# A streaming encoder layer on one core: tile 0's expert routing moved into the attention stage, conditioning vectors loaded as rows, one load of the final norm, h2 of tiles 5 to 7 from the router's buffer, tile 5 routed five slots later

## Chip, cores and metric

One core of a Trainium2 chip. The metric is the device time of one launch in microseconds, the median over repeated runs. Everything is float32. The engines are PE (matrix products), DVE (vector), ACT (scalar functions), POOL (general; here it issues the gathers) and SP (here it issues DMAs); each works through its own instruction list in order and waits on semaphores.

## What is computed

One layer over 1024 prompt tokens and 32 sample tokens, D = 1024, in nine tiles of 128 tokens (the ninth holds the 32 sample tokens):

```python
sh1, sc1, g1, sh2, sc2, g2 = split(silu(c) @ w_ada + b_ada)      # per request group
h  = rmsnorm(x, norm1) * (1 + sc1) + sh1
columns = h @ w_in                                               # 1024 x 3592, to both mixers
A  = gated DeltaNet(columns)          # 4 heads, chunked delta rule, depthwise convolution in front
B  = differential attention(columns)  # 4 heads, causal by chunks of 64
x1 = x + g1 * (concat(A, B) @ w_out)
h2 = rmsnorm(x1, norm2) * (1 + sc2) + sh2
# experts: 16384 single neurons, 8 product-key heads, 16 best each
q = h2 @ peer_wq;  scores = q . peer_keys (two halves of 128 keys per head)
idx, gate = best 16 of the 16 x 16 sums of the halves' best 16;  gate = softmax
y = sum over the 128 chosen of gate * gelu(u[idx] . h2) * v[idx]
out = rmsnorm(x1 + g2 * y, final_norm)
```

The outputs are the normalised rows, the new keys and values, and the DeltaNet and convolution states.

## The kernel before

**Stages.** `build` (line 2988) emits blocks that run one after the other: `condition` (line 120: modulation vectors, 1/rms of x, load of w_in into SBUF), `project` (257: h @ w_in and the convolution for tiles 0 to 4), `deltanet` (464, tiles 0 to 4), `attend_first` (2903: attention, w_out and x1 of tiles 0 to 4) and `stream` (2858). All engines meet at the end of a block, and SP then clears the block's semaphores.

**Condition.** SP loads c_prompt, c_sample, b_ada and norm1 column-wise (lines 148 to 151: element k*128 + p goes to partition p), then w_ada in 12 column blocks of 2.1 MB through three buffers (157). PE multiplies the two conditions with each block (229) and transposes the result into columns (220). ACT squares the tiles of x (176), and from the third block on loads w_in in eight row blocks of 128 x 3592 (198); the projection's first product waits for all eight (409), then runs over eight column groups of 512 (405; the eighth has 8 columns).

**Attention.** `Attention` (1012) and `Router` (1500) are written as generators, one per engine and part, that yield a due time in planner units before each piece; `weave` (981) merges them into one instruction order per engine. In `attend_first` head n of the 20 is due at 13 + 7.5 n, the store of x1 of tile tl (1138) at 37.5 units after its last head. SP's order holds the query and key rows of the next tile (1119), the DeltaNet rows (1125), x (1131) and that store. PE: transposes of queries and keys (1295, 1296), scores (1312), transposes of the probabilities (1333), values (1348), the output projection (1376). PSUM banks 2 to 7 are used.

**Stream.** `Experts` (1803) computes 8 x 128 + 32 slots, one expert per token in each: POOL gathers a row of u and of v per token (1867, 1870; 0.5 MB each, 5 and 8 buffers), DVE multiplies u with h2 and sums (2032), ACT applies gelu (1951) and builds a diagonal matrix of the coefficients (1941), PE adds diag x v to two PSUM banks (1986). Here due times are slots; PE runs four slots behind. Beside tiles 0 to 3's slots, other stages are woven in through `Stream` (2819), one after the other: routing of tiles 0 to 4; projection (slot 145), DeltaNet (292) and attention (427) of tiles 5 to 8; from slot 604 on routing of tiles 5 to 8. Stage n's instructions wait until SP has ended stage n - 1.

**Router**, per tile: SP loads x1 into `h2r` (1546), with the first tile of a stage also the keys (1548), modulation rows (1537) and peer_wq, 8.4 MB (1551). ACT, DVE and ACT normalise `h2r` in place (1586 to 1592), DVE scales and shifts (1687, 1690), SP stores it to `h2_scratch` (1556). PE transposes the keys once (1625) and h2 (1632), multiplies with peer_wq in four blocks (1655, banks 4 and 5) and the keys (1641, banks 2 and 3), ACT copies both results out (1600, 1605), DVE finds the best keys (1697 to 1717), the candidates (1725 to 1758) and the indices (1779 to 1789). `route_*` place step p of 128 of a route between its first and last slot, w0 + p (w1 - w0)/128. Tile 0 has the slots before 0, so all of it stands ahead of the first gather; tile t of 1 to 4 has 31.5 (t - 1) and 54 slots, tiles 5 to 8 the slots of the tile before, tile 5 from 604 to 640.

**Around a tile.** POOL loads h2 of the next tile from `h2_scratch` 16 slots ahead (1848); for tiles 0 and 5 to 8 ACT copies it to PSUM at the tile's first slot (1947). At the end of a tile POOL loads x1 into `x1e` (1886), ACT squares the sum into the same buffer (1961), then POOL loads final_norm there (1889) and DVE multiplies (2072).

## Time and profile before

| | us |
|---|---|
| median of 3 runs | 4339.26 (4335.96 to 4350.27) |
| the profiled execution's own time | 4341.6 |
| its span, first to last instruction | 4339.9 |
| conditioning, up to the projection's first matmul | 152.8 |
| attention of tiles 0 to 4, SP's first load of x to the last store of x1 | 650.1 to 861.1 |
| routing of tile 0, up to the first gather | 868.1 to 965.2 |
| slots and what is woven into them | 965.2 to 4339.9 |

The span runs from the first to the last instruction; the time adds start and end of the launch. Busy shares over the span: PE 78%, DVE 57%, POOL 53%, PE's weight loads 41%, ACT 25%. The DMA engines moved 1308 MB, 1127 MB of them on POOL's queue. The share of busy time is a mean over stages with different limits, so a part is to be read in its own stretch. The granted clock is that of PE; 1.00 is 2.4 GHz and 0.50 is 1.2 GHz.

### The profile page before, as it was taken

Reading aid. Unit: us, or ns where it says so; the run is one execution under the profiler, and the core shown is the slowest. Engines: PE = TensorE matmul, PEld = TensorE weight load, DVE = VectorE, ACT = ScalarE, POOL = GpSimd, SP = SyncE. Lnnn points to the kernel's source line nnn. Section 1 sums busy time; section 2 is a strip of 40 time slices with the busy share of each in tenths; the row PEclk is TensorE's granted clock in tenths of the full one; section 3 lists DMA queues with packets and bytes.
Section 4 is the critical chain, followed back from the end, with each engine's and each line's share of the span. In section 5 each row is a group of like instructions: output and inputs, shape, how many; then the busy total and the mean of one; then the engine's idle time right before and its main releaser. Section 6 shows DMA issues by size and latency. Waiting matters only on the chain.

```text
span 4339.9 us, 37765 instructions
## 1 busy us (share of the span) xinstructions
PE 3391.8 (78%) x11402; PEld 1785.9 (41%) x11402; DVE 2489.9 (57%) x5734; ACT 1106.3 (25%) x2931; POOL 2309.2 (53%) x2237
## 2 busy tenths in 40 slices
PE   6797877638888779987986789787697788778755
PEld 1343764335555334433553344335253344235222
DVE  0132644356888766546775577654756646745653
ACT  1122334212221244112332345322211121121111
POOL 0000310006666756676777676675766666666674
PEclk9899988869999889998998899998899899899898
DMA  9322211049888989999999999999999999999996
GB/s 363 132 106 100 103 60 56 29 149 356 317 322 321 364 314 368 401 374 359 339 365 355 375 350 339 347 341 367 335 376 371 365 388 370 361 384 360 359 355 263
DMA packets 387978, 1308.12 MB, mean 301 GB/s; under 512 B 51348, under 2 KB 55684, under 8 KB 385735
## 3 DMA queue, kind: packets, MB, share of 16 engines
q0 software_dynamic: 309808, 1127.00, 69.5%
q1 hardware_dynamic: 74904, 157.12, 9.9%
q10 hardware_dynamic: 3072, 21.66, 1.3%
q8 instruction: 92, 1.51, 0.1%
q14 instruction: 102, 0.84, 0.1%
HBM read 1270.94 MB, written 38.99 MB: 302 GB/s over the span
## 4 chain that ended last, share of the span: by engine, by line
PE 33%; POOL 13%; issue 12%; DMA 11%; DVE 8%; ACT 2%; another core or an unknown queue 1%; SPq 0%; DVEq 0%; ACTq 0%; POOLq 0%
PE PS L1986 21%; DMA ubuf<-in_peer_u,idx 8%; POOL vbuf L1870 7%; POOL ubuf L1867 6%; PE PS L1655 5%; DVE ubuf L2032 3%; PE PS L2310 2%; PE PS L1376 1%; PE PS L1312 1%; PE PS L2307 1%; DMA ckeys<-rest_scratch 1%; PE PS L1641 1%; ACT diag L1941 1%; PE PS L1348 0%
## 5 line engine op out<-in xcount | busy, mean ns | idle before, releaser
L1986 PE MATMUL PS<-vbuf,diag 128*128 128x512 f32 x3936 | 1979.7, 644 | 537.6 <-issue 247.2
L1870 POOL DMA_INDIRECT vbuf<-in_peer_v,idx x1024 | 1079.8, 1054 | 733.1 <-PE PS L1986 368.3
L1986 PEld LDWEIGHTS PS<-vbuf,diag 128*128 128x128 f32 x3936 | 766.1, 206 | 1488.2 <-issue 1174.9
L1867 POOL DMA_INDIRECT ubuf<-in_peer_u,idx x1024 | 1074.3, 1049 | 389.0 <-issue 301.7
L2032 DVE SCALAR_TENSOR_TENSOR ubuf<-ubuf,PS 128x1024 f32<-128x1024 f32 x544 | 662.9, 1220 | 560.3 <-DMA ubuf<-in_peer_u,idx 414.9
L2032 DVE SCALAR_TENSOR_TENSOR ubuf<-ubuf,h2e 128x1024 f32<-128x1024 f32 x512 | 624.6, 1224 | 393.4 <-DMA ubuf<-in_peer_u,idx 339.5
L1951 ACT ACTIVATE acts<-dots 128x2 f32<-128x2 f32 x528 | 107.1, 203 | 2013.5 <-DVE ubuf L2032 1207.7
L1941 ACT ACTIVATE diag<-ident,coef 128x128 f32<-128x128 f32 x984 | 339.1, 387 | 26.7 <-PE PS L1986 21.8
L1655 PEld LDWEIGHTS PS<-h2T,wq 128*128 128x128 f32 x2304 | 290.2, 194 | 96.5 <-issue 84.8
L1655 PE MATMUL PS<-h2T,wq 128*128 128x128 f32 x2304 | 292.9, 277 | 9.6 <-ACT h2T L1595 8.5
L405 PE MATMUL PS<-w_in_sb,hT 128*128 128x512 f32 (+1 forms) x640 | 252.8, 554 | 4.0 <-DVE hT L426 2.8
L405 PEld LDWEIGHTS PS<-w_in_sb,hT 128*128 128x128 f32 x640 | 116.2, 191 | 138.0 <-issue 137.0
L610 POOL MEMSET tri<- 128x128 f32 x1 | 0.2, 205 | 286.4 <-POOLq L99 286.4
L1376 PE MATMUL PS<-wout,mT 128*128 128x512 f32 x288 | 138.6, 618 | 8.7 <-ACT mT L1246 7.3
L1840 POOL DMA_DIRECT2D g<-modrows_scratch x2 | 1.3, 668 | 225.8 <-POOLq L99 225.8
L229 PE MATMUL PS<-wada,cS 128*2 128x512 f32 x192 | 92.0, 636 | 36.6 <-DMA wada<-in_w_ada 36.6
L2310 PE MATMUL PS<-wst,hT 128*128 128x512 f32 x256 | 119.3, 597 | 0.0
L1312 PE MATMUL PS<-KT,qz 128*128 128x512 f32 (+3 forms) x224 | 98.5, 555 | 10.5 <-DVE sc L1424 7.8
L1951 ACT ACT_TABLE_LOAD x81 | 103.9, 1283 | 1.3
L642 POOL TENSOR_TENSOR lb<-bm,lvl 128x512 f32<-128x512 f32 x35 | 51.0, 1490 | 90.5 <-PE PS L743 77.4
L2003 DVE TENSOR_TENSOR coef<-acts,gate 128x2 f32<-128x2 f32 x512 | 81.5, 159 | 26.8 <-ACT acts L1951 21.7
L2015 DVE SCALAR_TENSOR_TENSOR yacc<-vbuf,coef,yacc 128x1024 f32<-128x1024 f32 x68 | 87.4, 1285 | 2.4
(428 smaller groups left out, 3434.7 us busy)
## 6 DMA issues: line engine op xcount, KB each, us to landing
wada<-in_w_ada SPq DMA_DIRECT2D x12, 2048.0 KB, 18.6
wq<-in_peer_wq SPq DMA_DIRECT2D x8, 2048.0 KB, 11.4
ubuf<-in_peer_u,idx POOLq DMA_INDIRECT x1024
vbuf<-in_peer_v,idx POOLq DMA_INDIRECT x1024
...
```

The costliest lines, as they stand in the source:

```text
L229: last = pe.matmul(PS[0:2, 1 + n % 2, :], cS[:, :, k], wada[:, n % BUFS, k, :], start=(k == 0), stop=(k == DC - 1))
L405: last = pe.matmul(PS[:, n % 6, 0:w], hT[:, p, k, :], g["w_in"][:, k, c:c + w], start=(k == 0), stop=(k == DC - 1))
L1312: last = pe.matmul(SK[:, a:a + cw], qz[:, j, :], KT[:, h, c:c + cw], start=True, stop=True)
L1376: last = pe.matmul(PS[:, self.YB, :], mT[:, k, :], self.wout[:, k, c * 512:(c + 1) * 512], start=(k == 0), stop=(k == DC - 1))
L1655: last = pe.matmul(PS[:, self.QBANK[b % 2], j * P:(j + 1) * P], self.wq[:, c, n * P:(n + 1) * P], self.h2T[:, c, :], start=(c == 0), stop= ...
L1867: pool.indirect_dma_start(out=g["ubuf"][:, c % RU, :], out_offset=None, in_=d["peer_u"][0], in_offset=bass.IndirectOffsetOnAxis(ap=at, axi ...
L1870: pool.indirect_dma_start(out=g["vbuf"][:, c % RV_, :], out_offset=None, in_=d["peer_v"][0], in_offset=bass.IndirectOffsetOnAxis(ap=at, ax ...
L1941: act.activation(g["diag"][:, at % DIAGS, :], g["ident"][:, :], ACT.Copy, scale=g["coef"][:, n:n + 1]).then_inc(f["diag"], 1)
L1951: act.activation(g["acts"][:, of], g["dots"][:, of], ACT.Gelu).then_inc(f["gelu"], 1)
L1986: last = pe.matmul(PS[:, h, :], g["diag"][:, (at - 1) % DIAGS, :], g["vbuf"][:, c % RV_, h * 512:(h + 1) * 512], start=(n == 0), stop=(n = ...
L2032: dve.scalar_tensor_tensor(g["ubuf"][:, c % RU, :], g["ubuf"][:, c % RU, :], 1.0, h2, ALU.mult, ALU.mult, accum_out=g["dots"][:, lo + n:lo ...
L2310: last = pe.matmul(bank, self.hT[:, j, i * P:(i + 1) * P], self.w[:, order % 2, j, :], start=(j == 0), stop=(j == DC - 1))
```

## The change

1. `condition`: the four vectors are loaded as 72 rows of 128 into `vecs`, transposed by one PE instruction and copied by DVE. w_in is loaded in the projection's eight column groups, the first after the sixth w_ada step, and each product group waits for its own.
2. Tile 0 is routed by a `Router` of its own in `attend_first`, due from 5 units behind the store of tile 0's x1 for 110 units. It uses banks 0 and 1 (one for products, one for scores and key transposes) and holds two of the four blocks of peer_wq at a time; SP's part is `sync_of_one`. Buffers of `Attention` are cut to the tiles in use.
3. In the stream routing begins with tile 1 (stage 1, keys and peer_wq loaded there), due at 4 + 30.5 (t - 1), 52.5 slots long. Tile t from 5 on is routed from max(609, 128 (t - 1) + 4).
4. h2 of tiles 5 to 7 isn't stored; ACT copies it to PSUM from `h2r`, and SP loads the next x1 after that copy. Tile 8's h2 is stored as before.
5. final_norm is loaded once into `fnorm`. `acts` and `coef` become `dots`, `fold_s` becomes `gate_s`.

```diff
-            sp.dma_start(cT[:, 0, :], d["c_prompt"][0, :].rearrange("(k p) -> p k", p=P)).then_inc(ld_c, 16)
-            sp.dma_start(cT[:, 1, :], d["c_sample"][0, :].rearrange("(k p) -> p k", p=P)).then_inc(ld_c, 16)
-            sp.dma_start(bada[:, :], d["b_ada"][0, :].rearrange("(k p) -> p k", p=P)).then_inc(ld_b, 16)
-            sp.dma_start(n1T[:, :], d["norm1"][0, :].rearrange("(k p) -> p k", p=P)).then_inc(ld_b, 16)
+            row = 0
+            for name in ("c_prompt", "c_sample", "b_ada", "norm1"):
+                rows = d[name][0, :].rearrange("(k p) -> k p", p=P)
+                sp.dma_start(vecs[row:row + rows.shape[0], :], rows).then_inc(ld_v, 16)
+                row += rows.shape[0]
...
+            def columns_of_w_in(n):
+                cols = slice(n * GC, min((n + 1) * GC, IN_COLS))
+                act.dma_start(g["w_in"][:, :, cols], wi[:, :, cols]).then_inc(g["ld_win"][n], 16)
...
-                if 2 <= n < 2 + DC:
-                    act.dma_start(g["w_in"][:, n - 2, :], wi[:, n - 2, :]).then_inc(g["ld_win"], 16)
+                if n >= 5:
+                    columns_of_w_in(n - 5)
+            columns_of_w_in(7)
...
+            pe.wait_ge(ld_v, 64)
+            pe.transpose(PS[:, 3, 0:VECS], vecs[:, :], g["ident"][0:VECS, 0:VECS]).then_inc(v_psum, 1)
...
+            dve.tensor_copy(cT[:, :], PS[:, 3, 0:VECS]).then_inc(v_cols, 1)
...
+                    pe.wait_ge(g["ld_win"][n], 16)
...
-            pe.wait_ge(g["ld_win"], 16 * DC)
...
-ROUTE_STEP, ROUTE_LONG = 31.5, 54
+ROUTE_FROM, ROUTE_STEP, ROUTE_LONG = 4, 30.5, 52.5
...
+        weave(Between(None, 0), queries(), gdn_rows(), residual(), *([cached()] if self.t1 > NT else []), *more)
...
+    def first_loads(self, sp, blocks=4):
+        kv = self.d["peer_keys"][0].rearrange("h two n c -> n (h two) c")
+        sp.dma_start(self.sc[:, :, :], kv).then_inc(self.r["key_in"], 16)
+        self.rows_of(sp, 0)
+        for b in range(blocks):
+            self.load_weights(sp, b)
+
+    def load_weights(self, sp, b):
+        wv = self.d["peer_wq"][0].rearrange("(k p) c -> p k c", p=P)
+        at = self.wq[:, b % 2, :, :] if self.streamed else self.wq[:, :, b * 512:(b + 1) * 512]
+        sp.dma_start(at, wv[:, :, b * 512:(b + 1) * 512]).then_inc(self.r[f"wq{b}"], 16)
+
+    def sync_of_one(self, sp, stored):
+
+        r, (rt, w0, w1) = self.r, self.routes[0]
+
+        def at(p):
+            return w0 + p * (w1 - w0) / NSLOT
+
+        yield 0
+        self.first_loads(sp, 2)
+        yield stored
+        sp.dma_start(self.h2r[:, :], self.g["x1_scratch"][rt]).then_inc(r["x1_in"], 16)
+        yield at(15)
+        sp.wait_ge(r["h2_ready"], rt + 1)
+        sp.dma_start(self.g["h2_scratch"][rt], self.h2r[:, :]).then_inc(r["stored"], 16)
+        for b in (2, 3):
+            yield at(31 + 10 * (b - 2))
+            sp.wait_ge(r["q_psum"], 4 * rt + b - 1)
+            self.load_weights(sp, b)
+        yield at(114)
+        sp.wait_ge(r["stored"], 16 * (rt + 1))
+        sp.wait_ge(r["idx_ready"], rt + 1)
+        sp.wait_ge(r["gate_ready"], rt + 1)
...
-            some(sp, r["stored"], 16 * rt)
+            some(sp, r["stored"], 16 * kept_rows(rt - 1))
             some(sp, r["hT_psum"], rt)
+            if from_router(rt - 1):
+                sp.wait_ge(self.experts.f["h2_psum"], self.experts.in_psum_to(rt - 1))
...
+            if not from_router(rt):
+                sp.dma_start(g["h2_scratch"][rt], self.h2r[:, :]).then_inc(r["stored"], 16)
...
-                    some(pe, r["q_sb"], 4 * q + b - 1)
+                    some(pe, r["q_sb"], 4 * q + b - len(self.QBANK) + 1)
                 for c in range(DC):
-                    last = pe.matmul(PS[:, self.QBANK[b % 2], j * P:(j + 1) * P], self.wq[:, c, n * P:(n + 1) * P], self.h2T[:, c, :],
+                    last = pe.matmul(PS[:, self.QBANK[b % len(self.QBANK)], j * P:(j + 1) * P], self.weights(c, n), self.h2T[:, c, :],
...
+            if from_router(t):
+                return
...
-                yield end + 15
-                pool.wait_ge(f["square"], t + 1)
-                pool.dma_start(g["x1e"][:, :], d["final_norm"].partition_broadcast(P)).then_inc(f["fin_in"], 16)
+                if t == 0:
+                    yield end + 15
+                    pool.dma_start(g["fnorm"][:, :], d["final_norm"].partition_broadcast(P)).then_inc(f["fin_in"], 16)
...
+                if from_router(t):
+                    act.wait_ge(self.r["h2_ready"], t + 1)
+                    rows = self.router.h2r[:, :]
...
-            dve.wait_ge(f["fin_in"], 16 * (fi + 1))
+            dve.wait_ge(f["fin_in"], 16)
             dve.wait_ge(f["yn"], fi + 1)
-            dve.tensor_tensor(y, y, g["x1e"][:, :], ALU.mult).then_inc(f["yw"], 1)
+            dve.tensor_tensor(y, y, g["fnorm"][:, :], ALU.mult).then_inc(f["yw"], 1)
...
-        stage(0, lambda m: Router(nc, g, d, m, 0, [(0, -NSLOT, 0)] + [(t, ROUTE_STEP * (t - 1), ROUTE_STEP * (t - 1) + ROUTE_LONG) for t in range(1, FRONT)]))
+        stage(0, lambda m: Router(nc, g, d, m, 1, [(t, ROUTE_FROM + ROUTE_STEP * (t - 1), ROUTE_FROM + ROUTE_STEP * (t - 1) + ROUTE_LONG) for t in range(1, FRONT)]))
...
-        stage(0, lambda m: Router(nc, g, d, m, 1, [(t, max(ROUTE_AT, number(t - 1, 0)), number(t, 0)) for t in steady]))
+        stage(0, lambda m: Router(nc, g, d, m, 2, [(t, max(ROUTE_AT + 5, number(t - 1, 4)), number(t, 0)) for t in steady]))
...
-        rows = m.sb("mrows", [P, 2, 4, D])
+        stored = a.at(H - 1, 38.6)
+        route = (0, stored + 5, stored + 115)
+        router = Router(nc, g, d, m, 0, [route], ((0, 1), (0,), (1,)), streamed=True)
+        rows = router.wq[:, :, :, :].rearrange("p s (v k) c -> p s v (k c)", v=4)
...
+            a.sync(sp, [router.sync_of_one(sp, stored)])
+            weave(Between(None, 0), *a.scalar(act), *router.scalar(act))
+            weave(Between(None, 0), *a.tensor(pe), *router.tensor(pe))
+            weave(Between(None, 0), *a.vector(dve), *router.vector(dve))
...
+        g["acts"] = g["coef"] = g["dots"]
+        g["fold_s"] = g["gate_s"]
```

## Rows read from the trace of the kernel before

**Rows 1.** Busy time by stretch: length; PE, PEld, DVE, ACT, POOL; clock; DMA share; GB/s.
```profile
12.30:66.00 53.70, 37.80 (x96) 7.94 (x96) 0.00 (x0) 8.20 (x15) 0.00 (x0) 0.96 1.01 375
...
868.00:965.00 97.00, 39.85 (x312) 38.32 (x312) 56.13 (x211) 15.40 (x23) 1.30 (x2) 0.68 0.38 136
965.00:1390.00 425.00, 363.90 (x1678) 232.32 (x1679) 335.50 (x1060) 98.05 (x254) 265.68 (x259) 0.93 0.90 325
...
3080.00:3480.00 400.00, 307.28 (x843) 144.35 (x844) 241.72 (x574) 77.93 (x240) 270.79 (x280) 0.91 0.97 367
```

**Rows 2.** Timeline of conditioning and the projection's start: start and duration, engine, line, idle before.
```profile
2.57 9.70 SPq L151 DMA_DIRECT2D n1T<-in_norm  x1
...
12.31 88.12 SPq L157 DMA_DIRECT2D wada<-in_w_ada  x12
...
93.00 7.03 PE L229 MATMUL PS<-wada,cS 128*2 128x512 f32 x16 [2.19 <-DMA wada<-in_w_ada]
...
146.86 1.15 ACT L334 ACTIVATE xn<-xt,rstd 128x1024 f32<-128x1024 f32 x1 [14.64 <-DMA xt<-in_x_prompt]
...
152.84 17.37 PE L405 MATMUL PS<-w_in_sb,hT 128*128 128x512 f32 x35 [2.82 <-DVE hT L426]
```

**Rows 3.** Timeline of SP: the stores of x1 in attention, then tile 0's routing.
```profile
698.54 0.33 SPq L1138 DMA_DIRECT2D x_scratch<-x  x1
...
737.35 0.33 SPq L1138 DMA_DIRECT2D x_scratch<-x  x1
...
778.08 0.33 SPq L1138 DMA_DIRECT2D x_scratch<-x  x1
...
828.72 0.32 SPq L1138 DMA_DIRECT2D x_scratch<-x  x1
...
861.13 0.32 SPq L1138 DMA_DIRECT2D x_scratch<-x  x1
...
868.05 0.85 SPq L1548 DMA_DIRECT2D scr<-in_peer_keys  x1
```

**Rows 4.** Busy time by stretch, in attention of tiles 2 to 4.
```profile
720.00:740.00 20.00, 18.49 (x60) 9.21 (x59) 7.77 (x19) 3.71 (x12) 0.00 (x0) 0.99 0.11 40
740.00:780.00 40.00, 29.60 (x102) 16.74 (x100) 19.73 (x42) 15.23 (x42) 0.00 (x0) 0.91 0.13 45
780.00:830.00 50.00, 33.38 (x123) 18.98 (x123) 23.05 (x43) 17.13 (x45) 0.00 (x0) 0.89 0.07 21
```

**Rows 5.** Timeline of POOL in tile 0's routing.
```profile
903.96 0.54 POOL L1848 DMA_DIRECT2D h2e<-h_scratch  x1 [35.19 <-DMA h_scratch<-h2r]
965.19 1.02 POOL L1867 DMA_INDIRECT ubuf<-in_peer_u,idx  x1 [60.69 <-DVE idx L1789]
```

**Rows 6.** Timeline of PE in attention.
```profile
657.22 0.47 PE L1295 MATMUL PS<-ident,qk_rows 128*128 128x128 f32 x1 [1.61 <-DMA qk_rows<-rest_scratch]
...
716.21 3.78 PE L1376 MATMUL PS<-wout,mT 128*128 128x512 f32 x4 [0.69 <-ACT mT L1246]
...
720.90 1.88 PE L1376 MATMUL PS<-wout,mT 128*128 128x512 f32 x4
```

**Rows 7.** Groups of instructions, 868 to 965 us: count | busy us, mean ns | idle before.
```profile
L1655 PE MATMUL PS<-h2T,wq 128*128 128x128 f32 x256 | 30.8, 283 | 1.1 <-ACT h2T L1595 1.1
...
L1641 PE MATMUL PS<-keysT,qhT 128*128 128x128 f32 x32 | 4.3, 278 | 0.7 <-ACT qhT L1600 0.7
...
L1600 ACT ACTIVATE qhT<-PS 128x512 f32<-128x512 f32 x4 | 2.4, 597 | 17.9 <-PE PS L1655 17.9
```

**Rows 8.** Timeline of DVE in tile 0's routing, the start of the candidate part.
```profile
932.13 2.29 DVE L1725 TENSOR_TENSOR scr<-v 128x2048 f32<-128x2048 f32 x1
```

**Rows 9.** Timeline of DVE at the start of tile 5's routing.
```profile
2963.51 0.15 DVE L1680 TENSOR_SCALAR ssr<-ssr 128x1 f32<-128x1 f32 x1 [17.01 <-ACT h2T L1586]
```

**Rows 10.** Busy time by stretch, inside that wait.
```profile
2952.00:2957.00 5.00, 0.00 (x0) 0.00 (x0) 0.00 (x0) 0.00 (x0) 0.00 (x0) 0.50 1.05 330
```

**Rows 11.** Timeline of the kernel's last product.
```profile
4323.92 1.23 DVE L2072 TENSOR_TENSOR ye<-ye,x1e 128x1024 f32<-128x1024 f32 x1 [2.70 <-DMA x1e<-in_final_norm]
```

121 lines of the change are left out of this document (65 added, 56 removed).

## Prediction, before any run of the change

> **What bounds the kernel now.** I read four views: busy time by stage, the timeline around the places that the diff touches, the groups of instructions of those stretches, and who waited for whom. The stages stand behind each other with barriers between, so time saved in one before the stream comes off the end unless the next one takes it back.
>
> The conditioning stage loads 25.2 MB of w_ada (12 x 2.10), 14.7 MB of w_in and 4.3 MB of x. From 12.3 us on the DMA engines are full, 375 GB/s at a share of 1.01 [rows 1]. It starts late: SP needs 9.70 us to issue the column-wise norm1 load, so the first w_ada load goes out at 12.31, and the first projection matmul runs at 152.84 [rows 2]. Attention over tiles 0 to 4 is a chain through PE, DVE and ACT. Its five stores of x1 are 30 planner units apart and stand at 698.5, 737.4, 778.1, 828.7 and 861.1 [rows 3], so a unit is 1.3 us, 1.7 in the fourth tile. PE is busy for 18.5 of 20 us and 29.6 of 40 in its middle, DVE for 23.1 of 50 later [rows 4]. Then tile 0 is routed with nothing beside it: from 868.05 to the first gather at 965.19, where POOL had waited 60.69 us for the indices [rows 3, 5], DMA at a share of 0.38 [rows 1]. In the stream several things are nearly full at once: DMA 0.90 with DVE 336 of 425 us at first, DMA 0.97 at 367 GB/s later [rows 1].
>
> **The change part by part.** My sum goes against the profiled execution's own 4341.6 us (span 4339.9), 2.3 us above the median of the runs, 4339.26.
>
> 1. *Conditioning.* Four row-wise loads replace four column-wise ones. The three issues ahead of the slow one were done by 2.57 [rows 2], so a row-wise fourth should end near 2.9: the first w_ada load goes out 9.4 us earlier. PE then needs a transpose, a DVE copy and Silu before its first product; they lie beside the first w_ada load. w_in is loaded in eight column groups, from the sixth w_ada step on, and the projection waits group by group. All 44.2 MB at 385 GB/s take 115 us, so the last byte lands at about 118; but w_ada now lands before most of w_in. A w_ada step costs PE 7.03 us plus 0.3 of transposes [rows 2]: twelve steps from 11.5, with 4 us of low clock at the start and about 5 of DMA waits, end near 108. The projection's load of x is queued on ACT behind the last w_in group and lands, an estimate, 6 us after it, at 124; from there to the first matmul it is 6 us, as from 146.86 to 152.84 today [rows 2], so 130: **-22**. Bounds: -9 if only the earlier start remains, -26 if PE never waits. The eight waits per tile ask for what has long landed; a wait alone is not in the trace, so 0 to +3, I take 0.
>
> 2. *Tile 0's routing leaves the open.* From 868.05 to 965.19 are 97.1 us; POOL's two loads in front of the first gather stay, some 2 us: **-95**. What it held is 39.9 us of PE, 56.1 of DVE, 15.4 of ACT [rows 1] and 10.5 MB of loads, and all of it goes elsewhere.
>
> 3. *Into attention.* (a) SP issues keys (1.05 MB), rows (1.05) and two weight blocks (4.2) in front of tile 1's query rows on the same queue. At 868 such a queue took 36 us for 11.5 MB: the h2 store issued last let POOL go only at 903.96 [rows 3, 5]. That is 320 GB/s, so 6.3 MB hold the queue for 20 us, and PE already waits 1.61 us for these rows at 657.22 [rows 6]. PE takes its work in order, so tile 0's remaining heads are stuck behind this wait: +17 (0 if later loads overtake, 22 if none does). (b) Products and scores: 30.8 + 4.3 us of PE [rows 7], due in units 96 to 134, that is 729 to 779. PE is busy there for some 39 of 50 us [rows 4]; 39 + 35 = 74 is the least, and with 4 us of idle that nothing fills 78: +28 (15 to 35). (c) One bank each for products and scores, and for the keys' transposes, instead of two: each ACT copy of 0.60 us [rows 7] that was beside the next product now stands in front of it, eight times that matter: +5. (d) The norm chain and the key transposes make PE wait for ACT and DVE some ten times, and two table switches join: +8 (3 to 12). (e) DVE: the candidate part, from 932.13 [rows 8] to the first gather, is some 33 us, so the key search is the other 23 of the 56.1. The search falls mostly where PE is the limit, +2; the candidates fall into units 134 to 177 (779 to 844), where DVE is busy for about 27 of 65 us [rows 4]. It fits in sum, but instructions of 2.3 us stand in front of a softmax that PE waits for: +12 (6 to 25). Sum **+72**, bounds 27 and 97.
>
> On (c) the Trainium skill, Perfetto Trace Analysis, section Matmuls, speaks against the change: independent groups should rotate through different PSUM banks, so that emptying one lies beside the next group's matmuls. By it all twelve copies, of 0.60 us each in rows 7, would stand in PE's path, some 7 us instead of my 5, and the sum would be 2 us later.
>
> 4. *At the stream's start.* Routing of tiles 1 to 4 is a stage of its own and loads keys, rows and all of wq again, 10.5 MB, now beside the gathers of tile 0 instead of under the open routing. At 400 GB/s that is 26 us of DMA, where DMA has a share of 0.90 [rows 1]: **+24** (10 to 28). Slots 4 instead of 0, 30.5 instead of 31.5: 0, DVE work and deadline stay.
>
> 5. *Tile 5's routing five slots later.* Today DVE stands 17.01 us while keys land [rows 9], a wait that gelu, products and gathers are queued behind. But DMA is full meanwhile, share 1.05 [rows 10]: what stands still are the gathers, what runs are the weights, and those bytes must pass anyway. Five slots of work under the wait, at 3.2 us, would give 16; the same routing work in 31 slots takes back part: **-8** (0 to -16). Tiles 6 and 7 now load x1 only once h2 of the tile before is in PSUM, with four slots, some 12 us, for 0.5 MB: 0.
>
> 6. *Fewer transfers.* Seven final-norm rows inside the stream (3.7 MB) and three stores and loads of h2 (3.1 MB) go: 6.8 MB at 367 GB/s are 18 us if DMA alone were the limit; a share of 0.97 with PE at 307 of 400 us [rows 1] says about half: **-9** (0 to -18).
>
> 7. *The end.* The last product waits 2.70 us for the final-norm row [rows 11]; its other input is an ACT scaling of 128x1024, 1.15 us in rows 2, which it would still wait for: **-2**.
>
> Sum: -22 - 95 + 72 + 24 - 8 - 9 - 2 = -40; 4341.6 - 40 = **4301**.
>
> **Rivals.**
> *A, filled gaps.* Routing goes into PE's waits and keeps its clock up: the same four matmuls take 3.78 us after an idle stretch and 1.88 after work [rows 6], and the granted clock is 0.91 from 740 to 780 [rows 4], a mix of 1.2 and 2.4 GHz. Then (b) is 12, (e) 4, (d) 4, the queue 15: attention grows by 40, and the time is 4269. For it: 10 of 40 us idle there; against: 720 to 740 has 0.99 already, with 1.5 us idle. The Trainium skill, TensorE: Matmul & The Clock Gate, section HAM oscillation, says bursts parted by waits fall back to the low clock each time; the trace agrees where it stands, and by that rule A is the outcome.
> *B, SP's queue decides (slower).* SP takes its work in order too: its waits for h2 and for the products of blocks 0 and 1 stand in front of later query rows, and weight blocks 2 and 3 are issued only then, nine units before PE wants them. A block takes 7 us at 320 GB/s once it is issued, and SP comes to it late: PE waits 10 us twice, and three further sets of query rows come 10 us late: +50 on top of the 72, 4351, and up to 4360 with the stream's start at its bound. It decides once attention grows by more than 110.
> *C, the front gives only its start.* w_in merely moves behind w_ada, x for the projection is stuck behind it on ACT's queue: -9 instead of -22, 4314.
> *D, not beside attention.* The route is due from unit 79 to 189, attention's last store at 193; if DVE's part slips past that store, 24 of its 33 us stand open again: 4325.
>
> **How the numbers follow.** The forecast has 0.48, A 0.24, B 0.11, C 0.11, D 0.06. What a measurement here can tell from no change is about 0.3%, 13 us. The forecast's own range is 4275 to 4328; A's bounds reach 4245, B's 4360. With a fifth left out: 4250 to 4346. Faster by over 0.3% means under 4326: nearly all of A, most of the forecast and C, half of D: 0.78. Within 0.3%: 0.13. Slower: 0.09, nearly all B.
>
> **What would show it.** The first projection matmul near 130, not 152.84 (143 is C). Attention's first store of x1 some 17 later against the stage's start, with PE waiting about 17 us for tile 1's query rows. From first to last store 162.6 us now; about 215 if I am right, under 195 for A, over 255 for B. The first gather 2 us after the stream's start, DMA at 1.0 in its first 50 us. No 17 us on DVE before tile 5's routing. Wrong altogether, if tile 0's route is still open behind attention's last store, or if the stream from first to last gather changes by more than 25 us.

## The result and the profile after

The changed kernel takes 4311.68 us (median of 20 runs), the kernel before in the same rounds 4336.29 (20 runs): a ratio of 0.9941, 95% interval 0.9927 to 0.9954. By that ratio it is 25.6 us less, 20 to 32 by the interval (the two medians lie 24.6 apart); the forecast was 40 less. The profiled execution has a span of 4318.9 us against 4339.9, 21.0 less. Where they went is seen at marks of the two traces:

| mark, us from the span's start | before | after | after - before |
|---|---|---|---|
| first matmul of the projection | 152.84 | 138.95 | -13.9 |
| attention: SP's first load of x | 650.09 | 635.38 | -14.7 |
| attention: first store of x1 | 698.54 | 702.33 | +3.8 |
| attention: last store of x1 | 861.13 | 918.94 | +57.8 |
| first gather | 965.19 | 927.69 | -37.5 |
| last gather | 4296.05 | 4280.27 | -15.8 |
| end | 4339.9 | 4318.9 | -21.0 |

The timeline of PE in the changed kernel, in conditioning and at the second tile of attention (it answers to [rows 2, 6]):

```profile
16.03 15.95 PE L240 MATMUL PS<-wada,cS 128*2 128x512 f32 x32 [12.18 <-DMA wada<-in_w_ada]
...
106.91 7.03 PE L240 MATMUL PS<-wada,cS 128*2 128x512 f32 x16 [2.63 <-DMA wada<-in_w_ada]
...
138.95 2.05 PE L417 MATMUL PS<-w_in_sb,hT 128*128 128x512 f32 x2 [2.93 <-DVE hT L437]
...
660.93 0.47 PE L1306 MATMUL PS<-ident,qk_rows 128*128 128x128 f32 x1 [20.14 <-DMA qk_rows<-rest_scratch]
```

w_ada is through at 113.94, 17.7 us earlier than the 131.6 of before (122.87 + 8.72 there), but the projection starts only 13.9 us earlier: from the one to the other it is 25.0 us. The timeline of ACT says what lies between:

```profile
113.98 1.04 ACTq L190 DMA_DIRECT2D w_in_sb<-in_w_in  x2
...
120.95 0.81 ACTq L297 DMA_DIRECT2D xt<-in_x_prompt  x1
...
132.85 1.15 ACT L345 ACTIVATE xn<-xt,rstd 128x1024 f32<-128x1024 f32 x1 [18.29 <-DMA xt<-in_x_prompt]
```

The last two column groups of w_in are issued at 113.98, the projection's first x behind them at 120.95, on the same queue; ACT waits for it until 132.85. The fourth line of the PE fence is the wait of step 3a, 20.14 us for tile 1's query rows. The timeline of SP shows the queue that makes it, and the stores of x1 [rows 3]:

```profile
636.41 0.84 SPq L1554 DMA_DIRECT2D scr<-in_peer_keys  x1
637.29 4.83 SPq L1588 DMA_DIRECT2D rows<-modrows_scratch  x1
642.16 1.48 SPq L1562 DMA_DIRECT2D wq<-in_peer_wq  x2
...
650.83 22.91 SPq L1130 DMA_DIRECT2D qk_rows<-rest_scratch  x2
...
702.33 0.33 SPq L1149 DMA_DIRECT2D x_scratch<-x  x1
...
817.92 0.33 SPq L1149 DMA_DIRECT2D x_scratch<-x  x1
...
918.94 0.32 SPq L1149 DMA_DIRECT2D x_scratch<-x  x1
```

Keys, rows and weights stand in front of the query rows. The first store comes 66.95 us behind the load of x (48.45 before), and from first to last store it is 216.6 us (162.6). Busy time between the five stores (length; PE, PEld, DVE, ACT, POOL; clock; DMA share; GB/s), first of the kernel before, then of the changed one:

```profile
698.50:737.30 38.80, 29.34 (x95) 15.74 (x95) 17.89 (x46) 14.84 (x45) 0.00 (x0) 0.87 0.15 48
737.30:778.10 40.80, 30.53 (x107) 17.57 (x107) 20.53 (x46) 16.06 (x45) 0.00 (x0) 0.92 0.13 46
778.10:828.70 50.60, 34.04 (x127) 19.40 (x127) 23.64 (x45) 17.13 (x45) 0.00 (x0) 0.90 0.08 26
828.70:861.10 32.40, 22.55 (x65) 12.00 (x65) 6.43 (x13) 4.61 (x14) 0.00 (x0) 0.84 0.09 32
```

```profile
702.30:752.90 50.60, 39.14 (x167) 25.60 (x168) 20.52 (x50) 22.76 (x55) 0.00 (x0) 0.87 0.17 58
752.90:817.90 65.00, 56.33 (x341) 43.89 (x339) 30.52 (x109) 20.26 (x52) 0.00 (x0) 0.95 0.26 94
817.90:877.20 59.30, 41.95 (x135) 25.48 (x135) 47.84 (x164) 17.77 (x46) 0.00 (x0) 0.77 0.07 23
877.20:918.90 41.70, 24.18 (x65) 13.44 (x65) 23.38 (x38) 4.82 (x15) 0.00 (x0) 0.72 0.07 26
...
927.69:1046.66 118.97, 81.78 (x392) 54.85 (x393) 52.25 (x153) 24.98 (x62) 60.86 (x65) 0.83 0.99 386
1046.66:1366.17 319.51, 282.72 (x1299) 179.66 (x1297) 280.32 (x899) 78.00 (x197) 203.02 (x193) 0.96 0.91 322
```

From first to third store (tiles 1 and 2, counted from 0) the stretch grew by 36.0 us and PE's work by 35.6 (59.9 to 95.5): PE's idle time is nearly as long as before, 20.1 us for 19.7. Who was waited for changed, though, as the waits of PE in that stretch say (us in total, times, longest), before and after:

```profile
PE PS L1333 <- DVE sc L1446: 17.6, 6, 5.2
```

```profile
PE PS L1344 <- DVE sc L1457: 7.8, 2, 6.3
PE PS L1704 <- ACT qhT L1649: 7.4, 3, 3.2
PE PS L1674 <- ACT keysT L1630: 3.1, 3, 1.7
PE PS L1323 <- ACT keysT L1630: 0.7, 1, 0.7
```

DVE's softmax now costs PE 7.8 us instead of 17.6; 11.2 us of waits for ACT's copies of products and keys are new. From third to last store PE has only eight score matmuls of routing work (1.9 us); what is new there is DVE's, busy for 71.2 us instead of 30.1. Of the 18.0 us more, 8.5 are idle time of PE (34.9 instead of 26.4) and 9.5 busy time: apart from the scores it needs 64.2 us instead of 56.6 for the same attention, since its granted clock is 0.77 and 0.72 instead of 0.90 and 0.84, a mix of 1.2 and 2.4 GHz that holds more of the low level.

The indices of tile 0 are ready at 895.5, before attention ends, and the first gather starts 8.75 us behind the last store of x1 instead of 104.06. The last two lines of the fence after are the stream's first 32 slots and the other 96 of tile 0. The timeline of DVE in the changed kernel, at the stream's start, at tile 5's routing and at the last product (the last two answer to [rows 9, 11]), and behind it the stream's start of the kernel before:

```profile
940.46 1.22 DVE L2107 SCALAR_TENSOR_TENSOR ubuf<-ubuf,PS 128x1024 f32<-128x1024 f32 x1 [14.18 <-DMA ubuf<-in_peer_u,idx]
945.17 1.22 DVE L2107 SCALAR_TENSOR_TENSOR ubuf<-ubuf,PS 128x1024 f32<-128x1024 f32 x1 [3.48 <-DMA ubuf<-in_peer_u,idx]
...
2950.79 0.15 DVE L1729 TENSOR_SCALAR ssr<-ssr 128x1 f32<-128x1 f32 x1 [4.55 <-ACT h2T L1635]
...
2954.53 1.22 DVE L2107 SCALAR_TENSOR_TENSOR ubuf<-ubuf,h2e 128x1024 f32<-128x1024 f32 x1 [1.45 <-DMA ubuf<-in_peer_u,idx]
...
2958.50 1.23 DVE L2107 SCALAR_TENSOR_TENSOR ubuf<-ubuf,h2e 128x1024 f32<-128x1024 f32 x1 [2.74 <-DMA ubuf<-in_peer_u,idx]
...
4306.02 1.23 DVE L2147 TENSOR_TENSOR ye<-ye,fnorm 128x1024 f32<-128x1024 f32 x1 [1.29 <-ACT ye L2041]
```

```profile
969.72 1.22 DVE L2032 SCALAR_TENSOR_TENSOR ubuf<-ubuf,PS 128x1024 f32<-128x1024 f32 x1 [4.05 <-DMA ubuf<-in_peer_u,idx]
973.18 1.22 DVE L2032 SCALAR_TENSOR_TENSOR ubuf<-ubuf,PS 128x1024 f32<-128x1024 f32 x1 [2.23 <-DMA ubuf<-in_peer_u,idx]
```

The first slot is multiplied 12.8 us behind its gather instead of 4.5, and the next one follows 4.7 us later instead of 3.5. The wait ahead of tile 5's routing fell from 17.01 us to 4.55, the one ahead of the last product from 2.70 to 1.29.

### The profile page after: what moved, and what is told of

The parts are those of the page before. It is cut to its first block, busy times and chain, and to the rows that moved or that the text cites. A ratio compares the mean times of both kernels' runs of the same rounds, so it can differ in the third digit from the quotient of the medians.

```text
span 4318.9 us, 37786 instructions
## 1 busy us (share of the span) xinstructions
PE 3404.1 (79%) x11419; PEld 1795.8 (42%) x11419; DVE 2487.5 (58%) x5735; ACT 1112.7 (26%) x2936; POOL 2305.1 (53%) x2226
## 4 chain that ended last, share of the span: by engine, by line
PE 28%; POOL 15%; issue 12%; DMA 12%; DVE 7%; ACT 2%; another core or an unknown queue 2%; SPq 1%; DVEq 0%; ACTq 0%; POOLq 0%
PE PS L2060 18%; DMA ubuf<-in_peer_u,idx 8%; POOL vbuf L1938 8%; POOL ubuf L1935 7%; PE PS L1704 4%; DVE ubuf L2107 3%; PE PS L2385 1%; DMA wq<-in_peer_wq 1%; PE PS L1387 1%; PE PS L2382 1%; ACT diag L2010 1%; DMA ckeys<-rest_scratch 1%; DVE ti L1786 0%; PE PS L1690 0%
## 5 line engine op out<-in xcount | busy, mean ns | idle before, releaser
L1938 POOL DMA_INDIRECT vbuf<-in_peer_v,idx x1024 | 1097.7, 1072 | 743.6 <-PE PS L2060 416.2
L1935 POOL DMA_INDIRECT ubuf<-in_peer_u,idx x1024 | 1058.1, 1033 | 345.8 <-issue 296.7
L2025 ACT ACTIVATE dots<-dots 128x2 f32<-128x2 f32 x528 | 108.1, 205 | 2007.6 <-DVE ubuf L2107 1149.6
L2010 ACT ACTIVATE diag<-ident,dots 128x128 f32<-128x128 f32 x984 | 341.5, 389 | 24.6 <-PE PS L2060 16.4
L417 PEld LDWEIGHTS PS<-w_in_sb,hT 128*128 128x128 f32 x640 | 116.2, 191 | 138.0 <-issue 136.9
L2077 DVE TENSOR_TENSOR dots<-dots,gate 128x2 f32<-128x2 f32 x512 | 81.9, 160 | 24.4 <-ACT dots L2025 16.2
L2089 DVE SCALAR_TENSOR_TENSOR yacc<-vbuf,dots,yacc 128x1024 f32<-128x1024 f32 x68 | 87.4, 1285 | 2.4
```

Of the source, the lines that this page charges most:

```text
L417: last = pe.matmul(PS[:, n % 6, 0:w], hT[:, p, k, :], g["w_in"][:, k, c:c + w], start=(k == 0), stop=(k == DC - 1))
L1935: pool.indirect_dma_start(out=g["ubuf"][:, c % RU, :], out_offset=None, in_=d["peer_u"][0], in_offset=bass.IndirectOffsetOnAxis(ap=at, axi ...
L1938: pool.indirect_dma_start(out=g["vbuf"][:, c % RV_, :], out_offset=None, in_=d["peer_v"][0], in_offset=bass.IndirectOffsetOnAxis(ap=at, ax ...
L2010: act.activation(g["diag"][:, at % DIAGS, :], g["ident"][:, :], ACT.Copy, scale=g["coef"][:, n:n + 1]).then_inc(f["diag"], 1)
L2025: act.activation(g["acts"][:, of], g["dots"][:, of], ACT.Gelu).then_inc(f["gelu"], 1)
```

## The experiments

All twelve runs by marks, beside the two kernels (projection: its first matmul; D: distance from attention's load of x to the first store of x1; E: first to last store; slots' tiles by the starts of their first gathers; tiles 5 to 7 in sum). Times are medians, in brackets the number of runs.

| kernel | projection | D | E | first gather | tile 0 | tile 4 | tiles 5-7 | time |
|---|---|---|---|---|---|---|---|---|
| before | 152.84 | 48.5 | 162.6 | 965.2 | 422.0 | 457.5 | 1119.3 | 4336.29 (20) |
| changed | 138.95 | 67.0 | 216.6 | 927.7 | 438.5 | 451.3 | 1121.6 | 4311.68 (20) |
| e1 | 136.37 | 48.8 | 214.1 | 904.8 | 438.2 | 459.4 | 1129.7 | 4315.24 (5) |
| e2 | 131.24 | 67.1 | 214.4 | 917.1 | 437.7 | 455.7 | 1132.5 | 4320.26 (4) |
| e3 | 141.08 | 68.6 | 214.1 | 930.2 | 438.8 | 453.9 | 1131.5 | 4329.96 (1) |
| e4 | 138.64 | 66.8 | 198.6 | 909.2 | 440.4 | 451.5 | 1133.5 | 4309.02 (1) |
| e5 | 140.83 | 48.8 | 166.4 | 956.6 | 418.5 | 457.8 | 1136.4 | 4341.56 (10) |
| e6 | 137.77 | 67.5 | 214.4 | 924.8 | 438.4 | 454.2 | 1132.1 | 4328.22 (9) |
| e7 | 138.69 | 66.7 | 216.9 | 927.1 | 435.5 | 453.2 | 1132.4 | 4331.51 (1) |
| e8 | 131.43 | 48.5 | 214.0 | 900.1 | 439.0 | 451.4 | 1135.9 | 4310.91 (6) |
| e9 (changed again) | 138.38 | 68.8 | 214.1 | 926.3 | 439.9 | 451.5 | 1126.3 | 4307.23 (6) |
| e10 (e8 again) | 130.85 | 48.7 | 213.9 | 899.3 | 440.7 | 448.1 | 1120.0 | 4284.65 (6) |
| e11 | 131.31 | 50.1 | 214.2 | 900.1 | 455.6 | 447.4 | 1121.9 | 4300.48 (7) |
| e12 | 136.95 | 67.4 | 214.1 | 921.9 | 450.9 | 450.5 | 1125.8 | 4334.94 (1) |

Three groups of runs are in it: the kernel before had 4347.92 beside e1 to e4, 4353.18 beside e5 to e8 and 4337.39 beside e9 to e12. So times are compared within one of these groups, or as ratios; up to the first gather the marks of equal code agree within 2 to 3 us. In the stream the length of tile 0 agrees within 5 us in the ten profiles with the change that leave its loads and routes alone (all but e5, e11 and e12), that of tile 1 or tile 4 only within 11 to 13 and the sum of tiles 5 to 7 within 16: smaller differences there say little.

**e1: the query rows in front of the weights.**

```diff
-        yield 0
+        yield 27
         self.first_loads(sp, 2)
```

> The changed kernel with one edit: the first loads of tile 0's router (keys, modulation rows, two weight blocks, 6.3 MB) are issued by SP behind tile 1's query rows instead of in front of them. In the changed kernel PE waits 20.14 us for these rows at 660.93, and the first store of x1 stands 66.95 us behind SP's load of x (48.45 before). Theory 1, the queue's order makes this wait: the wait falls to about 1.6 us as in the kernel before, the first store comes 48 to 50 us after the load of x, everything behind it moves up, and the whole is 17 to 20 us faster than the changed kernel's 4311.7: 4293. Theory 2, the bytes make it and not the order: the engines are full with the weights anyway, tile 1's rows or the next loads are late in another place, and the first store is at most 6 us earlier; 4306 to 4312. Theory 3, a later tile takes it back, since tile 0's weights then arrive late for their products: first store 17 us earlier, but the distance from first to last store grows from 216.6 to over 228.

PE's wait for the rows, and SP's order, in this kernel:

```profile
640.24 0.47 PE L1306 MATMUL PS<-ident,qk_rows 128*128 128x128 f32 x1 [1.69 <-DMA qk_rows<-rest_scratch]
```

```profile
635.88 0.33 SPq L1130 DMA_DIRECT2D qk_rows<-rest_scratch  x1
636.42 0.84 SPq L1554 DMA_DIRECT2D scr<-in_peer_keys  x1
...
640.94 2.29 SPq L1562 DMA_DIRECT2D wq<-in_peer_wq  x2
```

The wait is 1.69 us, the first store 48.8 us behind the load of x, the distance to the last store not longer. Theory 1 holds as to the place: 18.2 us of the distance from the load of x to the first store go, for the same bytes in the other order. The time alone (ratio 0.992, 0.9887 to 0.9953) doesn't say whether they reach the end; e8 and e10 do.

**e2: the projection's first x on SP's queue.**

```diff
+            sp.wait_ge(zeros, 2)
+            sp.dma_start(xt[:, :], xr[0]).then_inc(dma["x_loaded"], 16)
...
-            act.wait_ge(zeros, 2)
-            load_x(act, 0)
```

> The changed kernel with one edit: the projection's first load of x is issued by SP instead of ACT, whose queue still holds the last two column groups of w_in (4.2 MB at most). In the changed kernel this load is issued at 120.95, the scaling that waits for it starts at 132.85, and the first projection matmul stands at 138.95. Theory 1, the load is held by the queue it is in: it lands 3 to 6 us after its issue, the first matmul comes at 130 to 133, and the whole is 6 to 9 us faster than the changed kernel, 4304. Theory 2, it is held by full DMA engines, whatever the queue: the landing stays at 11 to 12 us, the first matmul at 137 to 139, and the time at 4312.

The timelines of SP and ACT, load and scaling:

```profile
120.50 0.35 SPq L304 DMA_DIRECT2D xt<-in_x_prompt  x1
```

```profile
125.14 1.15 ACT L347 ACTIVATE xn<-xt,rstd 128x1024 f32<-128x1024 f32 x1 [11.02 <-DMA xt<-in_x_prompt]
```

It is landed and read 4.6 us behind the issue, with w_in still on its way in the other queue (the DMA share is 1.08 from 121 to 125 us in this run and 1.01 from 125 to 131): theory 1. The first matmul stands at 131.24, the 130 that step 1 had.

**e3: the vectors column-wise again, w_in in its new order.**

```diff
-                rows = d[name][0, :].rearrange("(k p) -> k p", p=P)
-                sp.dma_start(vecs[row:row + rows.shape[0], :], rows).then_inc(ld_v, 16)
+                rows = d[name][0, :].rearrange("(k p) -> p k", p=P)
+                sp.dma_start(cT[:, row:row + rows.shape[1]], rows).then_inc(ld_v, 16)
...
```

The cut part takes the transpose and the copy out.

> The changed kernel with the four vectors loaded column-wise again (no transpose, no copy) and w_in still in its eight column groups behind w_ada. It divides the 13.9 us that the conditioning stage gained into the earlier start and the other order of w_in. Theory 1, the earlier start counts with what the first block of w_ada shows, 4.5 us (its product starts at 16.03 instead of 20.54) and the order of w_in gives the other 9.4: first projection matmul at 143 to 144. Theory 2, the whole 10 us of SP's issue count: first matmul at 148 to 149. Theory 3, the order of w_in gives it all, since products of w_ada set the stage's end and the start is waited out again: 139 to 140.

```profile
20.34 16.82 PE L238 MATMUL PS<-wada,cS 128*2 128x512 f32 x32 [20.34 <-DMA wada<-in_w_ada]
...
111.91 8.55 PE L238 MATMUL PS<-wada,cS 128*2 128x512 f32 x16 [2.31 <-DMA wada<-in_w_ada]
...
141.08 4.60 PE L413 MATMUL PS<-w_in_sb,hT 128*128 128x512 f32 x5 [2.96 <-DVE hT L433]
```

This is the timeline of PE: first and last block of w_ada, first matmul of the projection. 141.1 stands between theories 1 and 3. Against 138.0, the mean of seven profiles that have part 1 unaltered in the changed kernel, the earlier start counts 3 us and the order of w_in 11 to 12. w_ada ends 6.5 us later than in the changed kernel (120.46), but from there to the first matmul it is 20.6 us instead of 25.0: with a later w_ada, less of w_in may be left in front of x, which wasn't followed.

**e4: a quarter of tile 0's products.**

```diff
-                for c in range(DC):
+                upto = 2 if self.streamed else DC
+                for c in range(upto):
...
-                                     start=(c == 0), stop=(c == DC - 1))
+                                     start=(c == 0), stop=(c == upto - 1))
```

> The changed kernel, but tile 0's products with peer_wq in the attention stage take two of the eight parts of the contraction: three quarters of them, 192 matmuls of 288 ns (26 to 27 us of PE), are left out, and the scores of tile 0 are therefore others. From the first to the last store of x1 it is 216.6 us in the changed kernel and 162.6 before. Theory 1 (the forecast's step 3b), PE sets the pace of tiles 2 and 3 and its added work counts nearly in full: the distance falls by 22 to 30 us, nearly all of it between the first and the third store (115.6 now). Theory 2, DVE or the chain between the engines sets the pace and the products lie in waits: it falls by less than 10. Theory 3, the products keep PE's clock up, and without them the clock falls and takes back half: by 10 to 18.

Busy time between its first three stores:

```profile
701.90:749.20 47.30, 35.78 (x135) 21.98 (x135) 20.44 (x49) 22.95 (x56) 0.00 (x0) 0.86 0.18 61
749.20:800.70 51.50, 39.89 (x180) 25.77 (x179) 30.13 (x110) 19.78 (x52) 0.00 (x0) 0.90 0.32 118
```

The stretch has 98.8 us instead of 112.7 to 115.8 in the kernels with all products, 14 to 17 less for 26 to 27 us of work left out, and the clock is 0.86 and 0.90 where it was 0.87 and 0.95: theory 3. PE sets the pace there, but some 10 to 12 of the 26 us (three quarters of the 35.1 us that these products keep PE busy in the changed kernel; they overlap, so their mean of 288 ns doesn't add up) come back. Against the changed kernel PE's busy time falls by only 19.8, from 95.5 to 75.7, and its idle time grows by 3.0, from 20.1 to 23.1. Against e3, of the same group and with all products, PE's busy time falls by 15.8, from 91.4, and the clock from 0.93 and 0.97: what is left runs at a lower clock.

**e5: part 1 alone, on the kernel before.** The edit is the first two items of the diff in front of the prediction.

> The kernel before with part 1 of the change alone: vectors loaded as rows, w_in in column groups behind w_ada. The first projection matmul is to stand at 136 to 139, as in the changed kernel, instead of 152.84. Theory 1, stages stand behind each other and what the front gains comes off the end: 14 to 16 us faster than before, ratio 0.9965. Theory 2, a later stage takes it back: under 5 us. The stream of this run is that of the kernel before, on the chip of these runs: with it the tiles of the changed kernel are compared. In the changed kernel from first to last gather it is 3344 to 3370 us in five profiles, 3330.9 in the one of before. If the stream is slower by the change, it is 3325 to 3338 here, tile 0 422 and tiles 5 to 7 1117 to 1122 in sum; if chip and day make that difference, 3340 or more, and tiles 5 to 7 1127 or more.

The ratio is 0.997 (0.9949 to 0.9991), 13 us of the 4353 beside it (4 to 22 by the interval), where the first matmul gained 12.0: what the front gains comes off the end, as theory 1 has it, though the interval's near end touches theory 2. The first matmul stands at 140.8, 2 us behind what was expected. The profiled execution lies some 20 us above the median of the ten, so its stream as a whole says little, but its tiles do: tile 0 takes 418.5, so the 435 to 441 us of the ten profiles with the change are the change's; tiles 5 to 7 take 1136.4, so that the 1120 to 1136 of the others are no difference.

**e6: the transfers back.**

```diff
 def from_router(t):
-    return FRONT <= t < NT
+    return False
...
-                if t == 0:
+                if True:
                     yield end + 15
+                    pool.wait_ge(f["square"], t + 1)
                     pool.dma_start(g["fnorm"][:, :], d["final_norm"].partition_broadcast(P)).then_inc(f["fin_in"], 16)
...
-            dve.wait_ge(f["fin_in"], 16)
+            dve.wait_ge(f["fin_in"], 16 * (fi + 1))
```

> The changed kernel with parts 4 and 5 undone as to traffic: h2 of tiles 5 to 7 is stored and loaded again, the final norm's row is loaded again for every tile, 6.8 MB more. Theory 1 (the forecast's step 6), the engines are nearly full and half of the time of these bytes counts: tiles 5 to 7 take 5 us more in sum than in the changed kernel (1122 to 1134 there in five profiles), the whole 9 us more, 0.2% slower than the changed kernel. Theory 2, the pace of tiles 5 to 7 isn't set by bytes: no difference over 3 us. Theory 3, taking h2 from the router's buffer costs more than it saves, since SP waits with the next load of x1 and the route starts later: tiles 5 to 7 get shorter by 5 to 10 in sum, 1115 to 1122.

Tiles 5 to 7 take 1132.1, beside 1132.4 and 1135.9 in the two others of the same chip that have the change; the ratio is 0.9942 (0.9919 to 0.9965), that of the changed kernel 0.9941. Theory 2: 6.8 MB less were worth nothing that shows. With tiles 5 to 7 that differ by up to 16 us between profiles and with ratios that leave some 10 us open, the 5 and 9 us of theory 1 aren't excluded by this run alone.

**e7: 14.7 MB more, all over the stream.**

```diff
...
+                if t < NT - 1:
+                    for j in range(4):
+                        yield end + 60 + 15 * j
+                        pool.wait_ge(f["fin_in"], 16 * (1 + 4 * t + j))
+                        pool.dma_start(g["fnorm"][:, :], d["final_norm"].partition_broadcast(P)).then_inc(f["fin_in"], 16)
```

> The changed kernel with 28 additional loads of the final norm's row (0.52 MB each, four in each of tiles 1 to 7, at slots 60, 75, 90 and 105, on POOL's queue): 14.7 MB, the price of bytes in the stream. In each of tiles 1 to 7 that is 2.1 MB. Theory 1, DMA alone sets the pace: 5.7 us a tile, 40 in sum. Theory 2 (the forecast's step 6), half: 2.9 a tile, 20 in sum. Theory 3, the pace is set by the latency of the gathers and by the buffers, and such loads find room: under 1 a tile, under 7 in sum.

Tiles 1 to 7 take 2841.1 us, beside 2831.6 (e6) and 2833.9 (e8) on the same chip: 7 to 10 us, 0.5 to 0.65 us for a MB where full engines would need 2.7. That excludes theory 1 and leaves theory 3 as the nearest, but no more: the same sum is 2842.9 in e1 and 2829.7 in e2, which have no such loads, so the price may be nothing. In tiles 5 to 7, which got 6.3 of the 14.7 MB and lie in the stretch with a DMA share of 0.97, the sum is 1132.4, beside 1132.1 and 1135.9: nothing shows there.

**e8 and e10: e1 and e2 together**, the same kernel twice, the second time beside the changed kernel itself (**e9**).

> The changed kernel with both edits that mended the front: SP issues the first loads of tile 0's router behind tile 1's query rows, and the projection's first load of x. Each alone moved the first gather, by 20.3 us (against the projection's first matmul) and by 7.4. Theory 1, they add up and come off the end: first gather at 897 instead of 925 to 930, ratio to before 0.988 (0.9941 less 27 us of 4340). Theory 2, the stream takes it back, as the first of them looked (first gather 23 us earlier, time only 0.2% under the changed kernel's ratio): ratio 0.991 to 0.994 with first to last gather 3360 or more.

> The changed kernel itself, unaltered, on the same chip and in the same rounds as the next two, so that they can be compared with it and not only with the kernel before. Expected: ratio to before 0.993 to 0.996 as the first time, first gather at 924 to 928, tile 0 of the stream 436 to 440 us, first to last gather 3350 to 3360.

> The two edits of the front once more, beside the changed kernel itself. Theory 1, the 25 us that the first gather comes earlier reach the end: 20 to 28 us faster than the changed kernel in the same rounds. Theory 2, the stream takes half or more back: under 13 us faster, with a stream longer by as much. The stream's instructions are the same in both, so theory 2 would need a state of the chip that goes with the earlier start.

The first time the ratio to before was 0.9911 (0.9879 to 0.9942), too wide to decide. The second time 4284.65 us stand against 4307.23 of the changed kernel and 4337.39 of the one before, in the same rounds: ratios of 0.9877 (0.9854 to 0.99) and 0.9927 (0.9902 to 0.9951) to before. Its first gather is 27.0 us earlier and it is 22.6 us faster, with no run of the one (4277 to 4292) as long as any of the other (4297 to 4317): theory 1, this version beats both kernels.

**e11: the loads of the stream's first routing stage spaced out**, on top of e8.

```diff
-ROUTE_FROM, ROUTE_STEP, ROUTE_LONG = 4, 30.5, 52.5
+ROUTE_FROM, ROUTE_STEP, ROUTE_LONG = 16, 28, 48
...
+            sp.wait_ge(self.experts.f["dotted"], 2)
...
+                sp.wait_ge(self.experts.f["dotted"], 5 + 5 * b)
             self.load_weights(sp, b)
```

> The two edits of the front, and the loads of the stream's first routing stage spaced out: SP waits for 2 slots before keys and modulation rows and for 5, 10, 15 and 20 slots before the four blocks of peer_wq; the route of tile 1 is due from slot 16 instead of 4, with a step of 28 and 48 slots each, so that tile 4 ends at slot 148 as before. In the changed kernel the first multiplication of the stream starts 12.8 us behind the first gather (4.5 before) and the next slots follow 3.98 us apart while the weights land (2.55 before). Theory 1, the 16 to 18 us that tile 0 lost are this share of the engines: gathers alone run first, the first multiplication comes 4 to 6 us behind the first gather, tile 0 takes 422 to 430 instead of 438 us, and the whole is 8 to 16 us faster than the two edits alone. Theory 2, the bytes must pass in any case and only move: tile 0 435 to 440, no gain. Theory 3, the routes, now closer together, make DVE the pace later: tile 0 faster, tile 1 slower by as much.

The timeline of DVE at its first two slots, and busy time of the first 32 slots and the other 96 of tile 0:

```profile
907.71 1.22 DVE L2112 SCALAR_TENSOR_TENSOR ubuf<-ubuf,PS 128x1024 f32<-128x1024 f32 x1 [9.04 <-DMA ubuf<-in_peer_u,idx]
910.17 1.22 DVE L2112 SCALAR_TENSOR_TENSOR ubuf<-ubuf,PS 128x1024 f32<-128x1024 f32 x1 [1.23 <-DMA ubuf<-in_peer_u,idx]
```

```profile
900.08:1009.27 109.19, 65.20 (x200) 33.42 (x201) 39.12 (x76) 21.21 (x54) 60.95 (x65) 0.81 1.03 409
1009.27:1355.66 346.39, 306.30 (x1485) 201.88 (x1484) 293.28 (x967) 83.05 (x208) 205.02 (x194) 0.95 0.86 303
```

The gathers do run first: the second slot comes 2.5 us behind the first, and 32 slots take 109.2 us instead of 118.2 in e10. But PE is busy for only 65.2 us there instead of 83.5, and the work that isn't done has to be done in the next 96 slots, where PE is busy for 306 of 346 us (284 of 322 in e10). Tile 0 takes 455.6 us, 15 more than in e10, and the whole 15.8 more. None of the theories had that: the third came nearest, but it is in tile 0 itself, and with PE as much as DVE. As loads and due times were moved together, their shares aren't told apart.

**e12: the weights moved twice.**

```diff
+        if self.stage == 1:
...
+            for b in range(4):
+                sp.dma_start(self.g["spare"][b], wv[:, :, b * 512:(b + 1) * 512]).then_inc(self.r["spare"], 16)
...
+            sp.wait_ge(r["spare"], 64)
```

SP waits for the copies only at the end of that routing stage.

> The changed kernel with peer_wq's four blocks moved a second time at the stream's start, behind the real loads on SP's queue, from memory to memory so that nobody waits for them: 8.4 MB more beside the first gathers. Theory 1 (the forecast's step 4), bytes beside the gathers of tile 0 cost their time at full engines: tile 0 takes 14 to 21 us more than the changed kernel's 438, 452 to 459. Theory 2, the 16 to 18 us of tile 0 come from PE and ACT waiting for the keys and the weights in order, not from bytes: tile 0 takes 438 to 443.

The timeline of SP and busy time of the same two stretches:

```profile
927.51 35.69 SPq L1566 DMA_DIRECT2D wq<-in_peer_wq  x4
963.25 59.03 SPq L1561 DMA_DIRECT2D spare_scratch<-in_peer_wq  x4
1022.32 13.88 SPq L1609 DMA_DIRECT2D h_scratch<-h2r  x1
```

```profile
921.87:1044.79 122.92, 83.19 (x392) 54.98 (x393) 45.29 (x123) 23.00 (x58) 60.94 (x64) 0.83 1.03 409
1044.79:1372.73 327.94, 287.31 (x1299) 180.75 (x1297) 287.35 (x929) 79.28 (x203) 202.07 (x194) 0.94 0.91 326
```

Tile 0 takes 450.9 us, 12 more than the mean of 438.7 in the ten profiles with the change that leave these loads and routes alone: 1.45 us for each of the 8.4 MB. That is just under the range of theory 1, but it isn't all a price of bytes. In the first 32 slots, in which the copies move, it is 122.9 us against a mean of 118.3: 4.6 us, 0.55 a MB. The other 7.6 us come in the next 96 slots (327.9 against 320.4), when the copies have landed, and there DVE has 7 us more to do (287.35 against 280.32 in the changed kernel), work that it didn't get to in the first 32 (45.29 against 52.25). The copies hold SP's queue for 59 us and push the store of tile 1's h2 from 53 us behind the first gather to 100, and SP's next load of x1 from 77 to 134, so the route of tile 2 is late. How the 12 us divide between bytes and later routes stays open.

## Why the prediction was right in direction and too large by 14

The time lies in the range and on the side of the forecast; the sum of -40 met -25.6 (-20 to -32). The gains that it had too large are those of the conditioning (step 1, by 8), of the transfers (step 6, by up to 9) and of tile 5's routing (step 5, by up to 8); step 4 cost 6 less than it said, which makes up for a part. By its steps:

1. *Conditioning, -22: -13.9.* The step's own mark, w_ada's last block, came at 113.9 and not 108; 4.5 of the 5.9 us are its first block, now loaded beside the first tiles of x, which was there at 16.0 and not 11.5. Of the 9.4 us earlier start 3 are left at the first matmul (e3). The term that was mis-sized is x: it was put at 6 us behind the last byte of w_in, 124, but is read at 132.85, 11.9 us behind its issue, which e2 shows to be the queue: with x on SP's queue the first matmul is at 130.9 to 131.4. Rival C's mechanism, x stuck behind w_in, was in the forecast with too small a price.
2. *Routing out of the open, -95: -95.3* (104.06 to 8.75 us between last store and first gather). Right.
3. *Into attention, +72: +72.5.* Step (a), SP's queue, 17: 18.5, and e1 shows that it is the order: with the query rows in front 0.3 us of it are left. Steps (b) to (d), products, one bank, norm chain and keys, 41: 36.0 from first to third store. Step (e), DVE, 14: 18.0 from third to last. The distance of the stores was put at about 215 and is 216.6 (214 in most other profiles with the change; 162.6 before, 166.4 in e5). So the sum fits, but in part by luck: 5 too much and 4 too little cancel. Inside (b) the reason was a little off: e4 says that leaving out 27 us of products gives only 14 to 17, so a part of rival A, filled gaps and a better clock, is true in tile 2, at 0.95 instead of 0.92 (0.97 in e3). In tiles 3 and 4 the clock went the other way, to 0.77 and 0.72, with DVE as the pace. Rival A as a whole (distance under 195) fell, and so did B (over 255) and D (the route done 23 us before attention's last store).
4. *Stream's start, +24: +16 to +20* in tile 0 (418.5 and 422.0 without, 435.5 to 440.7 with). The place and the sign were right, and all of it lies in the first 32 slots: 118.3 us in the mean of the ten, 97.1 and 99.6 without the change, the other 96 slots 320.4 beside 325.0 and 318.9. The step put the 10.5 MB at 400 GB/s, 2.5 us a MB; 18 us are 1.8. That the bytes alone are the reason isn't shown: e12 has only 0.55 to 1.45 a MB for such bytes, and in the first 32 slots PE, which takes its work in order, also waits 22.6 us for the keys and 13.8 for ACT's copy of them, waits that this stretch didn't have before, while POOL's gathers of v wait 33.3 us for PE instead of 19.6. No run has the loads without these waits.
5. *Tile 5 later, -8: nothing that shows.* The wait on DVE went as said, and as said the bytes pass anyway: the slots after it are 4.0 us apart while the weights land (2954.53 and 2958.50), and the 32 slots from 608 on take 141.5 in the mean of the ten profiles instead of 141.6 and 143.4, slots 600 to 650, which hold both versions of that routing's start, 195.1 instead of 192.9 and 196.1. Tile 4 as a whole takes 453.0 (448 to 459) instead of 457.5 and 457.8, but what is shorter are its slots before 600, ahead of this routing. The five slots were not taken back by a run of their own.
6. *Fewer transfers, -9: nothing that shows* (e6). This is the step whose reason failed: it took a DMA share of 0.97 to mean that the bytes set half of the pace, 1.3 us a MB. e7 put in 14.7 MB and by the profiles beside it they cost 0.5 to 0.65 us each MB, and nothing that shows in tiles 5 to 7; there is room under that share. At 0.65 the step would be -4.
7. *The end, -2: -1.4* at the last product; in e6, which loads the row there again, the wait is 2.41 us instead of 1.29. From last gather to end it is 5.2 us less; the rest lies mostly behind that product and wasn't followed.

At the first gather the sum of steps 1 to 3 is -45 against -37.5 measured, the missing 8 being step 1's. For the stream the steps gave +5 (4, 5, 6 and 7). What medians and marks give is 13 in the first runs (before, 4336.3 - 965.2 = 3371 us from the first gather to the end of the launch; changed, 4311.7 - 927.7 = 3384) and 9 beside e9 (3372 and 3381). That sum moves with the spread of a stream: from first to last gather it is 3352.6 us in the changed kernel's profile and 3344 to 3371 in the ten, 3330.9 before and 3359.4 in e5 with the stream of before. By the first pair it is 22 us longer, close to the 25 by which the forecast would have been wrong altogether; by e5 it isn't longer at all. So a remainder of some us isn't settled: tile 1 looks 6 us longer and tiles 2 and 3 together 8 shorter in the mean, with only two profiles of the stream without the change.

The Trainium skill, Perfetto Trace Analysis, section Matmuls, has independent groups rotate through different PSUM banks, so that emptying one lies beside the next group's matmuls. The waits of PE for the copies of products are 7.4 us in three waits, and 3.8 us for those of the keys: on this the trace agrees with the page rather than with the 5 us of step (c), though a wait of up to 3.2 us is more than a copy of 0.60, and no run has two banks. The Trainium skill, TensorE: Matmul & The Clock Gate, section HAM oscillation, has bursts of matmuls parted by waits that are long enough start at the low clock again each time. The trace agrees in the tiles where DVE became the pace (0.72), and in e4, where PE's gaps were opened again (0.90 for 0.95). That rival A would be the outcome by that rule, the measurement didn't bear out, for the work that filled PE's gaps in one tile opened others in the next.
